# Two of the decay mixer's input columns change places, GpSimd's second pair waits for VectorE, and TensorE's filler matmuls stand ahead of both recurrences

## The reference, cut to what matters

```python
feats = centred_token_shift(feats, mu)          # x + mu0*(x_prev - x) + mu1*(x_next - x)
r, k, v, wd, ad = split(feats)                  # 256, 256, 256, 64, 64 columns
...
xs = (r, decay, k_mod, v, kk, a*kk), forward and backward in time
def step(s, inp):                               # decay mixer, 4 heads of 64
    sa = einsum('nhij,nhj->nhi', s, -kk_t)
    s = s * w_t + sa * b_t + v_t * k_t
    y = einsum('nhij,nhj->nhi', s, r_t)
```

## Time and profile before

| | us |
|---|---|
| median of 3 runs | 2013.85 |
| lowest, highest | 2013.14, 2021.18 |
| the profiled execution | 2016.32 |
| its span, first to last instruction | 2014.5 |
| busy in the span: TensorE / VectorE / ScalarE / GpSimd | 1764.4 / 864.8 / 592.6 / 246.9 |
| mean granted clock of TensorE | 0.966 of full |

### The profile page before, as it was taken

The page is one execution under the profiler, slowest core; times in us unless marked ns, Lnnn a source line. Parts: engine busy times, 40 slices in busy tenths (PEclk is TensorE's granted clock), DMA queues, the critical chain, the costliest instruction groups (busy, mean ns, idle before and its releaser), DMA issues.

```text
span 2014.5 us, 44025 instructions
## 1 busy us (share of the span) xinstructions
PE 1764.4 (88%) x17970; PEld 1034.2 (51%) x17970; DVE 864.8 (43%) x1514; ACT 592.6 (29%) x1018; POOL 246.9 (12%) x270
## 2 busy tenths in 40 slices
PE   5998995977877877998998889999999997899996
PEld 2444543544443443447765774454448755753452
DVE  1667433211111111558656753160467657542331
ACT  3414520000000000343315424261253334323442
POOL 0002211111111111006204000001011103000001
PEclk9999997999999999999999999999999999999998
DMA  9767035999999998421000012110211000012101
GB/s 356 257 229 257 1 116 197 398 423 424 426 424 423 423 425 364 184 73 34 3 3 2 3 49 79 42 43 32 79 43 35 3 2 2 3 65 103 42 1 42
DMA packets 75098, 307.75 MB, mean 153 GB/s; under 512 B 10908, under 2 KB 22300, under 8 KB 57888
## 3 DMA queue, kind: packets, MB, share of 16 engines
q1 hardware_dynamic: 63280, 291.98, 37.0%
q0 software_dynamic: 5360, 9.33, 1.3%
q10 hardware_dynamic: 6272, 3.81, 0.7%
HBM read 301.01 MB, written 16.52 MB: 158 GB/s over the span
## 4 chain that ended last, share of the span: by engine, by line
PE 72%; DVE 13%; another core or an unknown queue 5%; ACT 4%; issue 3%; DMA 2%; ACTq 1%; DVEq 0%; POOL 0%; SPq 0%; POOLq 0%
PE bank L495 13%; PE bank L2243 11%; PE bank L2259 6%; PE bank L1022 5%; PE bank L524 5%; PE bank L531 4%; PE bank L2081 3%; PE bank L2165 3%; PE bank L993 2%; DVE arena L1588 2%; DMA arena<-w_gate 2%; PE bank L2093 1%; PE bank L2105 1%; ACT arena L1034 1%
## 5 line engine op out<-in xcount | busy, mean ns | idle before, releaser
L495 PE MATMUL bank<-hT,arena 128*128 128x512 f32 (+1 forms) x640 | 288.8, 607 | 3.8 <-ACTq L1035 2.4
L2243 PE MATMUL bank<-arena 128*64 128x256 f32 x1792 | 214.2, 396 | 68.5 <-remote 66.1
L524 PE MATMUL bank<-arena 64*64 64x64 f32 x6656 | 214.4, 220 | 21.7 <-DVE arena L1716 7.4
L524 PEld LDWEIGHTS bank<-arena 64*64 64x64 f32 x6656 | 202.5, 135 | 36.3 <-DVE arena L1716 10.5
L2243 PEld LDWEIGHTS bank<-arena 128*64 128x64 f32 x1792 | 133.8, 142 | 158.9 <-issue 108.4
L495 PEld LDWEIGHTS bank<-hT,arena 128*128 128x128 f32 (+1 forms) x640 | 123.1, 194 | 162.3 <-issue 157.8
L2849 DVE COPY arena<-bank 128x256 f32<-128x256 f32 x32 | 13.6, 425 | 329.4 <-PE bank L2251 329.4
L2259 PE MATMUL bank<-arena 128*64 128x512 f32 x448 | 104.0, 606 | 16.4 <-remote 16.4
L1022 PE MATMUL bank<-arena 128*128 128x512 f32 x256 | 110.4, 593 | 0.0
L1034 ACT ACTIVATE arena<-bank 128x512 f32<-128x512 f32 (+2 forms) x124 | 73.2, 590 | 120.8 <-PE bank L495 80.9
L531 PE MATMUL bank<-hT,arena 128*128 128x512 f32 x224 | 106.1, 612 | 0.0
(11 more groups left out here) (448 smaller groups left out, 2692.7 us busy)
## 6 DMA issues: line engine op xcount, KB each, us to landing
arena<-w_gate SPq DMA_DIRECT2D x28, 2048.0 KB, 30.7
arena<-w_up SPq DMA_DIRECT2D x28, 2048.0 KB, 20.9
arena<-w_down SPq DMA_DIRECT2D x28, 2048.0 KB, 26.1
arena<-w_ada SPq DMA_DIRECT2D x12, 2048.0 KB, 18.2
arena<-w_in SPq DMA_DIRECT2D x10, 2048.0 KB, 11.5
arena<-w_out SPq DMA_DIRECT2D x6, 2048.0 KB, 7.7
arena<-w_in SPq DMA_DIRECT2D x6, 1536.0 KB, 6.5
hT<-w_up SPq DMA_DIRECT2D x4, 2048.0 KB, 20.9
```

Source lines behind the costliest of these rows:

```text
L495: m = pe.matmul(bank[b][0:w, :], slot2(n)[:, k, c:c + w], hT[:, k, :], start=(k == 0), stop=(k == KD - 1))
L524: m = pe.matmul(o[half(f), s, t], lhs[half(f), s, t], rhs[half(f), s, t], start=True, stop=True)
L2243: mm = pe.matmul(bank[b][c * CAP:(c + 1) * CAP, 0:FE // 2], XT[j][:, k % 4, k // 4, :], e_slot(e_at(e, i), KD)[:, k, c * (FE // 2):(c + 1) ...
```

## The change

- **Columns 0 and 5 change places**, in the order of computing and in the weights: column 5's weights go to the first place of unit 3, column 0's to the second place of unit 4 (`PLACE`; the host permutes the weight columns). `fill` now makes columns 3, 4, 0; `shifted(5, 3)` stands where `shifted(0, 3)` stood. The receptance column 0 gets a tile of its own at another place.
- **VectorE** runs `decayed(0, 0)`, then the shift of column 5, then `decayed(0, 1)`. Value column 5 turns to token order within the first pair (bank 3).
- **GpSimd** waits for VectorE's second signal (after `decayed(0, 1)`) before its second pair.
- **VectorE's chunk stage** handles masks and set-up of direction 0, then those of direction 1.
- **The second pair's first direction** makes the products into banks 6, 7 first, and waits for ScalarE's copies (`uw_free`) only before those into banks 4, 5; VectorE waits for both halves at once there.
- **Both recurrences**: the wait for ScalarE's last copies moves from the end of the chunk stage to the recurrence. Ahead of it stand four filler matmuls in GDN; in the decay mixer the identity matmuls and sixteen value products, with six per step in place of eight.

```diff
@@ -406,9 +406,9 @@
         ra = Area(W0, arena, ARENA - T)
-        r_r, r_bon0, r_wa, r_kx, r_bon1, r_v = ra(2, T), ra(T), ra(1, T), ra(4, T), ra(T), ra(2, T)
-        r_bon = [r_bon0, r_bon1]
         ra.at += T
+        r_r1, r_bon0, r_wa, r_kx, r_bon1, r_v, r_r0 = ra(T), ra(T), ra(1, T), ra(4, T), ra(T), ra(2, T), ra(T)
+        r_bon, r_r = [r_bon0, r_bon1], [r_r0, r_r1]
         r_k, r_kk = r_kx[:, 0:2], r_kx[:, 2:4]
@@ -422,10 +422,11 @@
         assert ga.at <= ra.at - 9
-        RAW = (0, 1, 1, 2, 3, 4, 0)
+        RAW = (4, 1, 1, 2, 3, 0, 0)
+        PLACE = (5, 1, 2, 3, 4, 0, 6)
         LORA_BANK = (((3, 5), (4, 6)), ((2, 7), (0, 1)))
         def r_tile(i):
-            return r_wa[:, 0, :] if i == 6 else (r_r, r_k, r_v)[i // 2][:, i % 2, :]
+            return r_wa[:, 0, :] if i == 6 else r_r[i] if i < 2 else (r_k, r_v)[i // 2 - 1][:, i % 2, :]
         rx = Area(0, arena, 2 * UNIT)
@@ -528,7 +529,7 @@
                 for k in range(lo, hi):
-                    m = pe.matmul(bank[b][:, :], slot2(3 + i // 4)[:, k, (i % 4) * P:(i % 4 + 1) * P], hT[:, k, :],
+                    m = pe.matmul(bank[b][:, :], slot2(3 + PLACE[i] // 4)[:, k, (PLACE[i] % 4) * P:(PLACE[i] % 4 + 1) * P], hT[:, k, :],
                                   start=(k == 0), stop=(k == KD - 1))
@@ -620,17 +621,19 @@
                     m.then_inc(sem("g_w_done"), 1)
-                for d in range(2):
-                    uw_free[d].wait()
                 kk_free.wait()
...
                     n.clear()
-            def gdn_recurrence():
+                return uw_free
+            def gdn_recurrence(uw_free):
                 state, u_full = [[Count(pe, sem(f"{n}{d}")) for d in range(2)] for n in ("g_s_full", "g_u_full")]
...
                     for j in range(lo, hi):
-                        shifted(3 + j // KD, 6 + j // KD % 2, j % KD, j % KD + 1)
+                        shifted((3, 4, 0)[j // KD], 6 + j // KD % 2, j % KD, j % KD + 1)
+                fill(0, 4)
+                for d in range(2):
+                    uw_free[d].wait()
                 take(pe, sem("kd_full"))
@@ -642,7 +645,7 @@
                             m.then_inc(sem(f"g_ws_done{d}"), 1)
-                        fill(3 * n - 1, 3 * n + 1 if n < NC_G - 1 else 3 * KD)
+                        fill(3 * n + 3, min(3 * n + 5, 3 * KD))
                     for d in range(2):
@@ -654,7 +657,7 @@
                     if n < NC_G - 1:
-                        fill(3 * n + 1 if n else 0, 3 * n + 2)
+                        fill(3 * n + 5 if n else 4, 3 * n + 6)
                 for n in state + u_full:
@@ -684,8 +687,7 @@
                         take(pe, sem("v_ch_full"))
-                        for j in range(2):
-                            to_tokens(6 + j, r_v[:, j, :])
+                        to_tokens(6, r_v[:, 0, :])
             def rwkv_chunks():
@@ -693,14 +695,14 @@
                 for ct in range(2):
-                    if ct > 0:
-                        for d in range(2):
-                            uw_free[d].wait()
                     for d in range(2):
...
                             k_free.wait()
-                        for b, lhs in ((4, r_kmt), (6, r_bt)):
+                        for b, lhs in ((6, r_bt), (4, r_kmt)) if ct > d else ((4, r_kmt), (6, r_bt)):
+                            if ct > d and b == 4:
+                                for u in uw_free:
+                                    u.wait()
                             for t, f in pairs_in:
@@ -710,6 +712,9 @@
                         to_tokens(2, r_kmt[:, ct, d])
+                    if ct == 0:
+                        take(pe, sem("v_ch_full"))
+                        to_tokens(3, r_v[:, 1, :])
                     for d in range(2):
@@ -749,11 +754,10 @@
                     m.then_inc(sem("g_w_done"), 1)
-                for d in range(2):
-                    uw_free[d].wait()
-                for n in t_full + y_full + v_full + uw_free + [in_full, bt_full, k_free]:
+                for n in t_full + y_full + v_full + [in_full, bt_full, k_free]:
                     n.clear()
-            def rwkv_recurrence():
+                return uw_free
+            def rwkv_recurrence(uw_free):
 
@@ -781,6 +785,10 @@
                                   start=True, stop=False)
+                values_within(0, 16)
+                for u in uw_free:
+                    u.wait()
+                    u.clear()
                 for n in range(NC_G):
@@ -795,8 +803,7 @@
                             keys_values(d, t, f, 0)
-                    if n > 0:
-                        values_within(8 * n, 8 * n + 4)
+                    values_within(16 + 6 * n, 16 + 6 * n + 3)
                     for d in range(2):
@@ -809,7 +816,7 @@
                             m.then_inc(sem(f"g_inc_done{d}"), 1)
-                    values_within(8 * n + 4 if n > 0 else 0, 8 * n + 8)
+                    values_within(16 + 6 * n + 3, 16 + 6 * n + 6)
                     m = updates_within(n)
@@ -903,8 +910,7 @@
                         m.then_inc(for_dve[2], 1)
-                gdn_chunks()
-                gdn_recurrence()
+                gdn_recurrence(gdn_chunks())
                 o_free = Count(pe, sem("g_o_free"))
@@ -917,10 +923,9 @@
                 o_free.clear()
-                for ct in range(2):
-                    shifted(ct, 3 - ct)
-                rwkv_chunks()
-                rwkv_recurrence()
+                shifted(5, 3)
+                shifted(1, 2)
+                rwkv_recurrence(rwkv_chunks())
                 rwkv_outputs()
@@ -1189,8 +1194,8 @@
                 act.sem_inc(sem("wa_full"), 1)
-                for i in range(3, 6):
-                    raw(i, 6 + (i - 3) % 2)
+                for i, b in ((3, 6), (4, 7), (0, 6)):
+                    raw(i, b)
                 act.sem_inc(slot_free[0], 1)
@@ -1206,8 +1211,7 @@
                 output(1)
-                for i in range(2):
-                    to_tokens(6 + i, r_vtok[:, :, i * P:(i + 1) * P])
+                to_tokens(6, r_vtok[:, :, 0:P])
                 output(2)
@@ -1236,7 +1240,7 @@
                 decays(0, 0)
-                raw(0, 3)
+                raw(5, 3)
                 decays(0, 1)
@@ -1250,6 +1254,8 @@
                         act.sem_inc(sem("r_tok_full"), 1)
+                    if ct == 0:
+                        to_tokens(3, r_vtok[:, :, P:2 * P])
                     for d in range(2):
@@ -1408,6 +1414,8 @@
                 for ct in range(2):
+                    if ct == 1:
+                        take(pool, sem("kk_full"))
                     for e in range(2):
@@ -1632,7 +1640,7 @@
                 dve.sem_inc(sem("norm_in_full"), 1)
-                for i in (4, 5):
+                for i in (4, 0):
                     shift_both(i)
@@ -1675,16 +1683,18 @@
                     chain.mark(dve.scalar_tensor_tensor(kt, r_kk[:, ct, :], -1.0, kt, ALU.mult, ALU.mult))
-                    chain.mark(dve.tensor_tensor(rt, r_r[:, ct, :], rt, ALU.mult))
+                    chain.mark(dve.tensor_tensor(rt, r_r[ct], rt, ALU.mult))
                     km_full.wait()
...
                     decay_sums(0, d)
-                shift_both(0)
-                for d in range(2):
-                    decayed(0, d)
+                decayed(0, 0)
+                shift_both(5)
+                dve.sem_inc(sem("v_ch_full"), 1)
+                decayed(0, 1)
+                dve.sem_inc(sem("kk_full"), 1)
                 for ct in range(2):
@@ -1692,15 +1702,15 @@
                             return dve.tensor_tensor(pieces(dst), products[:, :, :, k, :], m, ALU.mult)
-                        k_done.wait()
+                        k_done.wait(2 if ct > d else 1)
                         chain(masked(r_BT[d], 4, 0, "excl"))
...
                         chain.mark(masked(r_PkT[:, ct, d], 4, 1, "incl"))
-                        k_done.wait()
+                        if ct <= d:
+                            k_done.wait()
                         bn_full.wait()
...
                         dve.sem_inc(sem("r_k_free"), 1)
-                    for d in range(2):
                         Y = r_kmt[:, ct, d]
@@ -1765,7 +1775,7 @@
                 for i in range(2):
-                    chain(dve.scalar_tensor_tensor(r_bon[i], r_bon[i], par2("r_k", i), r_r[:, i, :], ALU.mult, ALU.mult))
+                    chain(dve.scalar_tensor_tensor(r_bon[i], r_bon[i], par2("r_k", i), r_r[i], ALU.mult, ALU.mult))
                     dve.sem_inc(sem("bonus_full"), 1)
@@ -3027,6 +3037,9 @@
     w_in_cols = np.concatenate([cols[0:1792], cols[2456:2552], cols[2176:2200], cols[1792:2176], cols[2200:2456], cols[2552:]])
+    first, second = UNITS2[3][0], UNITS2[4][0] + P
+    w_in_cols = np.concatenate([w_in_cols[0:first], w_in_cols[second:second + P], w_in_cols[first + P:second], w_in_cols[first:first + P],
+                                w_in_cols[second + P:]])
     head = np.arange(MH)[:, None] * QK_M
```

## The result

Four runs of the changed kernel took 1994.73 to 2003.05 us, median 1999.66; the kernel before, run beside it, had a median of 2016.24 (four runs). The ratio is 0.9913, with a 95% interval of 0.9894 to 0.9932: 0.87% faster, about 17.5 us. The prediction had 1998.7 on 2013.85, a ratio of 0.9925.

The account below looks back on a forecast made before the run. TensorE holds 72% of the span; gains were sought at three places where others are busy. 0.2 + 6.4 + 0.2 + 0.8 = 7.6 us a layer, 15.2 for two, took 2013.85 to 1998.7; range 1991 to 2007.

Parts of the forecast that it names:

- the preparation: Decay mixer, from direction 0's last decay factor to the pair's inverse; forecast 6.4 us a layer shorter on average.
- GpSimd's second pair held back and the exchange: Decay mixer's preparation: direction 1 scaled without GpSimd, column 0 ready earlier; 6.4 us a layer, bounds about 2 and 8.2.
- VectorE now starts at 1668.6 rather than 1672.05.: Decay mixer's preparation, second layer: with columns exchanged, VectorE starts scaling direction 0 right at the first decay factors.
- The second rival: Decay mixer's preparation: only the held-back pair (4.1) and the recurrence's 0.8 count; 9.8 us for two layers, 2004.1; chance 0.06.
- But nine clears stay: Decay mixer's recurrence front: matmuls and value products move ahead of the copies' end, clears remain; 0.8 us, bounds 0 and 1.7.
- Fillers ahead: GDN recurrence: four matmuls move to the front; start 1.0 to 2.0 late, end 2.2 us back; 0.2 taken, bounds -0.5 and 1.2.
- The slower rival: Decay mixer's first pair: TensorE stays at 1.2 GHz through five levels, 10.5 us a layer more; 2022.9 us; chance 0.04.
- The second pair: Decay mixer: products not needing banks 4 and 5 run during ScalarE's last copies; 0.2 us, between 0 and 1.1.
- rest: Stage from VectorE's first state of the decay mixer to the normalization; no gain of its own in the forecast sum.

## Why the prediction held, and which terms did not

The time and the range held; the sum was right in the mechanism of its largest term and wrong in the make-up of the others. That the median came within 1 us is partly luck: the preparation gave 1.0 and 0.7 us less than forecast, the other stages 3.8 and 2.3 more. The stages gained 19.5 us against 15.2 forecast; the profiled execution came out at 13.3 by differences in work that the change doesn't touch, and the medians differ by 16.6.

*GpSimd's second pair held back and the exchange: 6.4 forecast, 5.4 and 5.7 measured.* The mechanism is as written: direction 1 in 2.5 us, masks free beside GpSimd, set-up blocked, products at 19.4 us for 19.6. In the second layer the set-up was blocked for 1.8 us (0.46 in direction 0, 0.36 + 0.95 in direction 1), in the first for 0.7, where I counted 2.8 and the rule of the Trainium skill (SBUF — State Buffer, section "Who interferes with whom") would allow 5.1. The rule itself agrees: three of the four set-up operations waited, none for longer than one of GpSimd's instructions, and once it was GpSimd that lost (1.28 us for 0.77), which I had left open. That the products came hardly earlier than forecast all the same (19.4 us) has its reason in where the blocking fell. The block of 1.1 us at L1686 was in the sum (1.3). Direction 0's set-up lost 1.5 us less than I counted, but that hardly shortened the chain, since direction 1's set-up then waits for ScalarE's evictions (0.48 us) and lost 1.3 where I counted 0.8. What made 6.8 us at the products into 5.7 behind them in the second layer is the clock; in the first it took 1.6 us out of direction 1's products.

*"VectorE now starts at 1668.6 rather than 1672.05."* True, and worth 0.4 of it: VectorE's work up to the masks is the same in either order, and the early start met GpSimd. The second rival, "the exchange does nothing on the path", was nearly right in what it says of the exchange, though by another way: not a wait for GpSimd's values, but a multiply blocked beside GpSimd's last instruction. Its time was not right, since the preparation as a whole (5.4 and 5.7 against its 4.1) and the other terms gave more.

*"But nine clears stay": the step that failed.* At both fronts my sum has the clears run ahead of the moved matmuls (fillers "near 1609.2", products done "near 1761.0"), and books them as a cost that stays, so that the gain seems to come from the matmuls. The runs show the opposite: the clears out from behind the wait are worth 1.17 us at the GDN front and 1.3 at the decay mixer's, and the moved matmuls 0.06 there. The second error of that term is the price of the identity matmuls, 1.76 us: their row stands in a stretch at 0.51 of the clock, and at full clock they take 1.10. So 0.8 was forecast, with an upper bound of 1.7, and 2.0 and 2.6 came.

*Fillers ahead: 0.2 forecast, 0 in the second layer.* The start is 1.95 late, as forecast (2.0), and the end is as forecast; but without the fillers the clears alone would have given 1.2. What I took for a small gain is a loss of 1.2 from the fillers that hides a gain of 1.2 from the clears.

*The clock.* The slower rival occurred in small: 1.2 us a layer, not 10.5, since the clock was back before the third product in the second layer, and before the levels began in the first. The argument against it, that 2.5 us idle is shorter than 5.5, did not hold as an argument: it fell behind gaps of 2.8 and 1.7 us in one layer and behind one of 2.8 alone in the other.

*The second pair*: 0.2 forecast, 0.4 and 0.5 measured, 0.3 of it by the directions' order. The other steps of the decay mixer ("rest") gained 1.0 and 0.3 that I gave nothing. With only the clears moved they gained 0.6 and 0.7 (16.65 / 16.40), so the moved matmuls aren't needed for it; but it also varies between kernels with the same steps (16.26 to 16.74), and no run takes it further apart.

## What to carry to other kernels

Semaphore clears and other bookkeeping belong ahead of the wait that ends last: here that alone, with the clock that it kept up, was worth about 5 us a layer in the kernel before, about half of it the clears themselves, where the matmuls moved with them gave 0.06 at one front and, as four fillers, lost 1.2 at the other. Where one engine is alone on the chain, hold back what slows it and has slack, and then look where the held work lands: released one step later it cost what it had saved. Work put ahead of a wait pays only while its removal shortens the other end; two fillers did, the third and fourth didn't.

## What the runs showed of the hardware that I had not expected

A semaphore clear in TensorE's queue behind a wait costs about 0.12 us (1.17 us for ten and a wait). TensorE's granted clock fell behind gaps of 2.8 and 1.7 us between bursts, once behind one of 2.8 alone (to 0.51), in seven of ten readings of the same order of work and not in the other three, and with unused matmuls in the gaps it stayed at full in both layers of two kernels. An fp32 operation of VectorE with both inputs in SBUF took 0.9 to 1.8 us instead of 0.69 where it started behind one of GpSimd's; where it started ahead, GpSimd's took 1.28 instead of 0.77. Beside GpSimd a scan took 1.70 instead of 1.18 and a copy of eight columns 1.06 instead of 0.17, while a stream transpose (0.71) and a product with an operand in PSUM (0.71) do not notice it.
